# A two-layer sparse-attention step on one core: other places for the threshold rounds, and the softmax reciprocals spread by PE instead of multiplied in by a diagonal

## The chip, the core and the metric

The kernel runs on one core of a Trainium2 chip. Its engines are PE (matrix products; PEld is its weight load), DVE (the vector engine), ACT (the scalar engine, with its function tables), POOL (the general engine) and SP (which issues transfers). Each works through its own list of instructions in order and waits on semaphores that the others raise. The metric is the device time of one execution in microseconds, the median of several.

## The reference

The reference is one step of a two-layer model for a prompt of 528 tokens (16 of them meta tokens) and 8 decoding sequences of 4 tokens with 2048 cached tokens each. The first layer is the one that matters here:

```
s     = einsum(qi, kidx);  score = einsum(relu(s), wi);  score = -inf beyond qpos
idx   = top_k(score, topk)                 # 132 keys of a prompt row, 256 of a decoding row
p     = softmax(q . k[idx] * 64**-0.5);  o = p @ v[idx]      # 8 heads of 64, 2 key heads
y     = concat(o, pooled) @ w_out          # pooled: moving averages over 2, 4, 8, 16 rows
```

A gated feed-forward follows, then a second layer with gated linear attention and another feed-forward. Outputs are the activations, new keys and values, and states.

## The kernel before

All matrix products run in float32 accuracy: each weight slab (RAW) is split into a high part by ACT (`hi`, WHI) and the rest by POOL (`lo`, WLO), and a product is three passes, `tile_rows` (L1820). A slab gives two tiles of 128 output columns, each of 8 steps over the inner dimension; a step is 6 matmuls.

The change lies in the first layer, from some 115 to 350 us of the span, in four stages.

Top-k and slab stage. DVE finds the prompt's top keys by 17 rounds, each of four `top8` (L1324) and four `take8` (L1330), one pair for each block of 112 rows. The decoding rows go another way: a threshold is searched bit by bit, in 32 rounds. A round is a count on DVE (`seek_count`, L1360, over all scores), a sum of the counts over partitions on PE (`row_total`, L1966, one matmul call, two instructions), and an update of the tried bits on DVE (`seek_update`, L1378 and L1380). Round r's count needs the update that reads total r-1. From the top-k round 10 on, DVE's list holds three such rounds in each top-k round (21 in all, `SEEK_EARLY`). At the same time PE works at slabs 4 to 7 (8 tiles, 64 steps), and its list holds total r behind step 3r+2. Ahead of tiles 0 to 5 stand three transposes (`kv_rows`), ahead of tile 6 four others. POOL's splits of slabs 6 and 7 (L607) fall in this stage.

Key phase. For y = 0 to 15, PE turns two chunks of cached keys (`k_turn`, L2010, 8 transposes), and multiplies the chunk turned before with the decoding queries (`k_logits`, L2026); ACT copies the turned keys (L974). Totals 21 to 32 stand one each in y = 1 to 12. Total 33 serves the choice among equal scores (`sample_mask`), and lies behind the first unit's logits; totals from 33 on use another PSUM bank than the others.

Prompt attention. 20 units n = 0 to 19, by descending row block i (n // 4 counts down from block 4 to block 0) and head pair p. A unit has `logits(n)` on PE (L2068), `row_max(n)` on DVE (L1447, adds the mask and takes the maximum), `exps(n)` on ACT (L992, with row sums), `scale_rows(n)` on DVE (L1462 the reciprocals of the sums, L1466 two diagonal matrices INV from identity and reciprocals), `flip(n)` on PE (L2086: each block of probabilities times INV, which turns and normalizes it at once, two instructions a block), `pt_copy(n)` on ACT (L1004), `values(n)` on PE (L2100), `o_hi(n)` on ACT (L1014) and `o_lo(n)` on DVE (L1475). Logits and probabilities are held twice, so units overlap. What overlaps is set by the order written out for each engine:

```
PE   n:  flip(n)  logits(n+2)  sample_masks  values(n)  pooled
ACT  n:  o_hi(n-1)  pt_copy(n)  exps(n+2)  pooled_hi
DVE  n:  scale_rows(n+1)  o_lo(n-1)  row_max(n+2)  pooled_lo  sample_mask  sample_max
```

`pooled` (L2117) and its two halves (`pooled_hi` L1019, `pooled_lo` L1481) are the moving averages' products; they stand in units 4, 5, 7, 8, 10, 11, 13 and 14. The masks of the decoding rows stand in units 12 to 18. POOL makes the moving averages beside this stage (L726 to L739), and its split of the output slab (`lo_at(out0, 0, 0)`, L613) comes behind the fetch of the fifth cached value block.

Of the kernel before, what the change touches and what calls it, by code (L numbers as in the profile page):

```python
# [32 lines left out]
P = 128  # L33
# [49 lines left out]
SEEK_EARLY, SEEK_FROM = 21, 10  # L83
# [12 lines left out]
CUT_STEPS = 5 + 2 * 31 + 3  # L96
# [76 lines left out]
def trunk(nc, t, o):  # L173
# [4 lines left out]
    with ExitStack() as ctx:  # L178
# [78 lines left out]
        INV, _, inv_end = region("INV", [RB, 2, 2, RB], F32, uo_end)  # L257
# [88 lines left out]
        def halved(ap):  # L346
# [22 lines left out]
        tk, nm_ready, nm_final, tks, nms_ready, newscore = (sem(n) for n in ("tk", "nm_ready", "nm_final", "tks", "nms_ready", "newscore"))  # L369
        part_count, row_count = (sem(n) for n in ("part_count", "row_count"))  # L370
        kvr_tr, kvr_ready, ue_tr, sp_ready, uo_ready = (sem(n) for n in ("kvr_tr", "kvr_ready", "ue_tr", "sp_ready", "uo_ready"))
        u_zero, pool_step, pd_ready, y_done, yhi, ylo = (sem(n) for n in ("u_zero", "pool_step", "pd_ready", "y_done", "yhi", "ylo"))
        lg_ready, mx_ready, exp_done, tail_done, p_ready, pt_tr, pt_evac, pv_done, ohi, olo = (
            sem(n) for n in ("lg_ready", "mx_ready", "exp_done", "tail_done", "p_ready", "pt_tr", "pt_evac", "pv_done", "ohi", "olo"))
# [222 lines left out]
        def _(pool):  # L597
# [95 lines left out]
            pool.memset(UE[:, :, 0:PB], 0.0).then_inc(u_zero, 1)  # L693
# [107 lines left out]
        def _(act):  # L801
# [141 lines left out]
            for s in range(6, 8):  # L943
                hi(s + 1)
                for j in range(2):
# [7 lines left out]
                    if g == 0:  # L953
                        act.wait_ge(u_zero, 1)
# [13 lines left out]

            for y in range(16):
# [254 lines left out]
        def _(dve):  # L1224
# [121 lines left out]
            def seek_count(r):  # L1346

                x, junk = SS[:, :], MET[:, :]
                if r == 0:
# [3 lines left out]
                    dve.tensor_tensor(new, new, VNF[3 * NS:P, 0:NS], ALU.mult).then_inc(newscore, 1)  # L1353
                    dve.wait_ge(newscore, 1)
                    dve.tensor_tensor(new, new, VNF[3 * NS:P, NS:2 * NS], ALU.add).then_inc(newscore, 1)
                    dve.wait_ge(newscore, 2)
# [5 lines left out]
            def total(r):  # L1362

                return PS[:, 7 if r < 33 else 1, 0:1]
# [46 lines left out]

            for r in range(1, ROUNDS_P):
# [14 lines left out]
            assert 3 * (ROUNDS_P - SEEK_FROM) == SEEK_EARLY  # L1427
# [29 lines left out]
            def scale_rows(n):  # L1457
# [4 lines left out]
                dve.reciprocal(ST[0:m, 1, 2 * n:2 * n + 2], ST[0:m, 2, 2 * n:2 * n + 2]).then_inc(p_ready, 1)  # L1462
                dve.wait_ge(p_ready, 2 * n + 1)
                if n >= 2:
                    dve.wait_ge(pt_tr, n - 1)
                dve.tensor_tensor(INV[0:m, n % 2, :, 0:m], IDN[0:m, 0:m].unsqueeze(1).to_broadcast([m, 2, m]),  # L1466
                                  ST[0:m, 1, 2 * n:2 * n + 2].unsqueeze(2).to_broadcast([m, 2, m]), ALU.mult).then_inc(p_ready, 1)
# [341 lines left out]
        def _(pe):  # L1809
# [153 lines left out]
            def row_total(r):  # L1963

                pe.wait_ge(part_count, r + 1)
                pe.matmul(PS[:, 7 if r < 33 else 1, 0:1], (PRIOR if r == 33 else SAME)[:, :, :].rearrange("p q n -> p (q n)"), SEEK[:, 2:3], start=True, stop=True).then_inc(row_count, 1)  # L1966
# [526 lines left out]
```

## Time and profile before

| | us |
|---|---|
| median of 3 executions | 1711.35 |
| lowest and highest | 1710.86, 1729.72 |
| the profiled execution's own time | 1712.0 |
| its span, first to last instruction | 1710.2 |
| PE busy in the span | 1589.6 (93%) |
| DVE, ACT, POOL busy | 544.1, 554.1, 549.9 (32% each) |

Shares are of the whole span, over stages with different limits. A row of the timeline gives start, duration, engine, line, operation, and in brackets the idle time ahead of it with what ended it. PEclk is the granted clock of TensorE as a share of 2.4 GHz; 0.50 is its lower level, 1.2 GHz.

### The profile page before, as it was taken

Reading aid. Unit: us, or ns where it says so; the run is one execution under the profiler, and the core shown is the slowest. Engines: PE = TensorE matmul, PEld = TensorE weight load, DVE = VectorE, ACT = ScalarE, POOL = GpSimd, SP = SyncE. Lnnn points to the kernel's source line nnn. Section 1 sums busy time; section 2 is a strip of 40 time slices with the busy share of each in tenths; the row PEclk is TensorE's granted clock in tenths of the full one; section 3 lists DMA queues with packets and bytes.
Section 4 is the critical chain, followed back from the end, with each engine's and each line's share of the span. In section 5 each row is a group of like instructions: output and inputs, shape, how many; then the busy total and the mean of one; then the engine's idle time right before and its main releaser. Section 6 shows DMA issues by size and latency. Waiting matters only on the chain.

```text
span 1710.2 us, 28405 instructions
## 1 busy us (share of the span) xinstructions
PE 1589.6 (93%) x11984; PEld 1484.9 (87%) x11984; DVE 544.1 (32%) x1089; ACT 554.1 (32%) x745; POOL 549.9 (32%) x206
## 2 busy tenths in 40 slices
PE   6896998898999999999889889999989999999996
PEld 6864866578999999999888887789989999999996
DVE  5269855632210101012316772233430111001113
ACT  4243245542432322223344332102333432222231
POOL 5410212513433343333354431002334333434240
PEclk9858998889999999999889987658989999999998
DMA  5322231132222223212221200034212222232221
GB/s 151 130 90 83 71 126 51 48 127 74 72 76 92 74 80 99 94 60 77 82 75 58 67 26 1 1 124 159 75 50 87 85 67 91 87 99 74 71 77 53
DMA packets 116840, 136.04 MB, mean 80 GB/s; under 512 B 5848, under 2 KB 111594, under 8 KB 114705
## 3 DMA queue, kind: packets, MB, share of 16 engines
q1 hardware_dynamic: 112949, 113.91, 21.2%
q0 software_dynamic: 3456, 20.97, 3.5%
q8 instruction: 58, 0.95, 0.2%
q14 instruction: 21, 0.17, 0.0%
q10 hardware_dynamic: 356, 0.03, 0.0%
HBM read 127.14 MB, written 7.94 MB: 79 GB/s over the span
## 4 chain that ended last, share of the span: by engine, by line
PE 84%; DVE 8%; ACT 4%; issue 2%; POOL 0%; ACTq 0%; DMA 0%; DVEq 0%; POOLq 0%
PE PS L1820 66%; PE PS L1917 2%; PE PS L2338 2%; PE PS L2375 2%; PE PS L2336 2%; DVE SC L1330 1%; DVE M L1324 1%; PE PS L2086 1%; PE PS L2370 1%; PE PS L2354 1%; PE PS L2304 1%; PE PS L1848 1%; PE PS L2010 1%; PE PS L2317 1%; DVE BC L1629 1%
## 5 line engine op out<-in xcount | busy, mean ns | idle before, releaser
L1820 PE MATMUL PS<-HHI,WHI 128*128 128x280 f32 x2304 | 647.8, 298 | 19.0 <-DVE HLO L1252 10.8
L1820 PE MATMUL PS<-HLO,WHI 128*128 128x280 f32 x2304 | 641.9, 295 | 0.0
L613 POOL TENSOR_TENSOR WLO<-RAW,WHI 128x2048 fp32r<-128x2048 f32 (+2 forms) x89 | 365.5, 4107 | 780.2 <-ACT WHI L825 590.4
L1820 PE MATMUL PS<-HHI,WLO 128*128 128x280 f32 x2304 | 489.9, 295 | 0.0
L1820 PEld LDWEIGHTS PS<-HHI,WHI 128*128 128x128 f32 x2304 | 444.2, 193 | 24.7 <-issue 14.8
L1820 PEld LDWEIGHTS PS<-HLO,WHI 128*128 128x128 f32 x2304 | 443.6, 193 | 0.0
L1820 PEld LDWEIGHTS PS<-HHI,WLO 128*128 128x128 f32 x2304 | 373.3, 192 | 0.0
L825 ACT ACTIVATE WHI<-RAW 128x2048 fp32r<-128x2048 f32 x87 | 166.1, 1909 | 149.0 <-PE PS L1820 146.0
L1820 PE MATMUL PS<-ALO,WHI 128*128 128x280 f32 x704 | 192.8, 291 | 0.0
L1820 PE MATMUL PS<-AHI,WHI 128*128 128x280 f32 x704 | 192.8, 291 | 0.0
L1595 DVE TENSOR_TENSOR AT<-PS,SG 128x560 f32<-128x560 f32 x44 | 32.6, 742 | 473.7 <-PE PS L1820 473.7
L1820 PE MATMUL PS<-AHI,WLO 128*128 128x280 f32 x704 | 147.5, 291 | 0.0
L1820 PEld LDWEIGHTS PS<-AHI,WHI 128*128 128x128 f32 x704 | 132.5, 188 | 0.0
L1820 PEld LDWEIGHTS PS<-ALO,WHI 128*128 128x128 f32 x704 | 132.3, 188 | 0.0
L1568 DVE TENSOR_TENSOR XT<-PS,XT 128x560 f32 x48 | 35.6, 742 | 298.0 <-PE PS L1820 298.0
L1820 PEld LDWEIGHTS PS<-AHI,WLO 128*128 128x128 f32 x704 | 111.7, 188 | 0.0
L607 POOL TENSOR_TENSOR WLO<-RAW,WHI 128x2048 fp32r<-128x2048 f32 x16 | 75.9, 4747 | 94.2 <-ACT WHI L818 87.8
L1107 ACT ACTIVATE AHI<-AT 128x560 f32 x44 | 29.6, 673 | 224.5 <-DVE AT L1595 224.5
L1102 ACT ACTIVATE SG<-PS 128x560 f32<-128x560 f32 x44 | 28.1, 639 | 147.8 <-PE PS L1820 147.4
L850 ACT ACTIVATE NRM<-XT 128x560 f32 (+1 forms) x32 | 21.5, 672 | 126.4 <-DVE XT L1568 126.2
L818 ACT ACTIVATE WHI<-RAW 128x2048 fp32r<-128x2048 f32 x18 | 34.4, 1911 | 26.2 <-PE PS L1820 24.5
L1917 PE MATMUL PS<-KID,QIT 64*112 64x112 f32 (+3 forms) x128 | 34.7, 554 | 5.8 <-ACT RL L898 5.1
(327 smaller groups left out, 1674.1 us busy)
## 6 DMA issues: line engine op xcount, KB each, us to landing
RAW<-in_ffn_w_gate SPq DMA_DIRECT2D x22, 1024.0 KB, 5.2
RAW<-in_ffn_w_up SPq DMA_DIRECT2D x22, 1024.0 KB, 5.3
RAW<-in_ffn_w_down SPq DMA_DIRECT2D x16, 768.0 KB, 4.7
RAW<-in_w_in_odd SPq DMA_DIRECT2D x12, 1024.0 KB, 5.3
RAW<-in_ffn_w_down SPq DMA_DIRECT2D x16, 640.0 KB, 4.2
RAW<-in_w_in_even SPq DMA_DIRECT2D x7, 1024.0 KB, 5.3
RAW<-in_w_out_even SPq DMA_DIRECT2D x4, 1024.0 KB, 5.2
SIN<-in_state_gla SPq DMA_DIRECT2D x8, 512.0 KB, 3.9
```

The costliest lines, as they stand in the source:

```text
L607: pool.tensor_tensor(WLO[:, s % 2, 0:kc, :], RAW[:, s % 2, 0:kc, :], WHI[:, s % 2, 0:kc, :].bitcast(F32), ALU.subtract).then_inc(lo_done, 1)
L613: pool.tensor_tensor(WLO[:, par, 0:kc, :], RAW[:, par, 0:kc, :], WHI[:, par, 0:kc, :].bitcast(F32), ALU.subtract).then_inc(lo_done, 1)
L818: act.activation(WHI[:, s % 2, :, :], RAW[:, s % 2, :, :], ACT.Copy).then_inc(hi_done, 1)
L825: act.activation(WHI[:, s % 2, :, :], RAW[:, s % 2, :, :], ACT.Copy).then_inc(hi_done, 1)
L1107: act.activation(AHI[:, ds(2 * i + j, 1), :].rearrange("p a n -> p (a n)"), AT[:, j, :], ACT.Copy).then_inc(ahi_ready, 1)
L1568: dve.tensor_tensor(x, halves(j), x, ALU.add).then_inc(acc_free[j], 1)
L1595: dve.tensor_tensor(halved(AT[:, j, :]), halves(j), halved(SG[:, j, :]), ALU.mult).then_inc(acc_free[j], 1)
L1820: ins = pe.matmul(acc[a][:, half, 0:HALF], w[:, slot, k, c0:c0 + P], x[:, k0 + k, HALF * half:HALF * half + HALF], start=first and n == 0 ...
L1917: ins = pe.matmul(PS[0:m, 4 + 2 * (n % 2) + half, 0:nk // 2], QIT[lo:lo + 64, h // 2, RB * i:RB * i + m], KID[lo:lo + 64, half * (nk // 2) ...
L2336: pe.matmul(out, STATE[:, c % 2, h, 128 * e:128 * e + 128], G[:, h, CH * c:CH * c + m], start=True, stop=False)
L2338: ins = pe.matmul(out, VR[rows, c % 2, x:x + 128], ATT[rows, h // 2, CH * c:CH * c + m], start=not inter, stop=True)
L2375: ins = pe.matmul(PS[:, 7, y:y + DT], SIN[:, b % 2, h, 128 * e:128 * e + 128], G[:, h, WP + DT * b:WP + DT * b + DT], start=True, stop=True)
```

## The change

Fourteen threshold rounds stay in the top-k rounds (two in each from round 10 on), and their totals lie further apart in the slab stage; the rest goes to the key phase. The flips become plain transposes, which need the exponentials only. The reciprocals are spread by PE: the column of a head's reciprocals, broadcast to 64 columns, is the weight, the identity streams, and 64 partitions get the reciprocal of each row. DVE copies that to SBUF (`spread`) and multiplies the product of the values with it (`o_norm`), ahead of `o_hi`. Logits of unit n+2 wait until `spread(n)` has read the bank that they share. An Exp on one column is put ahead of the key phase on ACT. POOL's split of the output slab goes behind the last fetch of cached values.

```diff
-SEEK_EARLY, SEEK_FROM = 21, 10
+SEEK_EARLY, SEEK_FROM = 14, 10
+SEEK_STEPS = [7 + 9 * r // 2 for r in range(13)]
+K_TOTALS = [[r for r in range(len(SEEK_STEPS), 33) if (r - len(SEEK_STEPS)) * 4 // 5 == y] for y in range(16)]
@@ gpsimd
-            cached("v", 4)
+            for b in range(4, 8):
+                cached("v", b)
             lo_at(out0, 0, 0)
-            for b in range(5, 8):
-                cached("v", b)
@@ scalar
+            act.activation(STS[:, 0, 0:1], IDN[:, 0:1], ACT.Exp)
             for y in range(16):
...
-                act.wait_ge(pv_done, n + 1)
+                act.wait_ge(o_rows, n + 1)
                 act.activation(HHI[:, p, RB * i:RB * i + m], PS[:, 2, 0:m], ACT.Copy).then_inc(ohi, 1)
@@ vector
                     if r >= SEEK_FROM and i == 3:
-                        seek_round(3 * (r - SEEK_FROM))
+                        seek_round(2 * (r - SEEK_FROM))
                 for i in range(1, NRB):
                     take8(i, 8 * r + i)
-                    if r >= SEEK_FROM and i % 2 == 0:
-                        seek_round(3 * (r - SEEK_FROM) + i // 2)
+                    if r >= SEEK_FROM and i == 3:
+                        seek_round(2 * (r - SEEK_FROM) + 1)
...
+            def row_inverse(n):
+                dve.wait_ge(exp_done, n + 1)
+                dve.reciprocal(ST[0:m, 1, 2 * n:2 * n + 2], ST[0:m, 2, 2 * n:2 * n + 2]).then_inc(rinv, 1)
+            def spread(n):
+                dve.wait_ge(inv_rows, n + 1)
+                if n >= 2:
+                    dve.wait_ge(o_rows, n - 1)
+                dve.tensor_copy(INV[:, n % 2, 0:m], PS[:, 4 + 2 * (n % 2), 0:m]).then_inc(rinv, 1)
+            def o_norm(n):
+                dve.wait_ge(rinv, 2 * n + 2)
+                dve.wait_ge(pv_done, n + 1)
+                dve.tensor_tensor(PS[:, 2, 0:m], PS[:, 2, 0:m], INV[:, n % 2, 0:m], ALU.mult).then_inc(o_rows, 1)
...
-            dve.wait_ge(nm_ready, NRB - 1)
+            sample_left()
+            sample_mask(2)
             row_max(0)
-            sample_left()
             row_max(1)
-            scale_rows(0)
+            row_inverse(0)
             for n in range(len(UNITS)):
-                if n + 1 < len(UNITS):
-                    scale_rows(n + 1)
+                spread(n)
                 if n:
                     o_lo(n - 1)
                 if n + 2 < len(UNITS):
                     row_max(n + 2)
                 if n in POOLED_AT:
                     pooled_lo(*POOLED_AT[n])
-                if n < 4:
-                    sample_mask(2 + n)
+                if n < 3:
+                    sample_mask(3 + n)
                 for k in MASKS_AT.get(n, ()):
                     sample_max(k)
+                if n + 1 < len(UNITS):
+                    row_inverse(n + 1)
+                o_norm(n)
@@ tensor
                         step = KC * tile + k
-                        if step % 3 == 2 and step // 3 < SEEK_EARLY:
-                            row_total(step // 3)
+                        if step in SEEK_STEPS:
+                            row_total(SEEK_STEPS.index(step))
...
-                if 1 <= y <= 32 - SEEK_EARLY + 1:
-                    row_total(SEEK_EARLY + y - 1)
+                for r in K_TOTALS[y]:
+                    row_total(r)
...
                 k_logits(y)
+            pe.wait_ge(tks, CUT_STEPS)
+            row_total(33)
...
-                pe.wait_ge(p_ready, 2 * n + 2)
+                pe.wait_ge(exp_done, n + 1)
...
-                        ins = pe.matmul(PS[0:kb, j // per, c:c + m], PR[0:m, n % 2, x, RB * j:RB * j + kb], INV[0:m, n % 2, x, 0:m], start=True, stop=True)
+                        ins = pe.transpose(PS[0:kb, j // per, c:c + m], PR[0:m, n % 2, x, RB * j:RB * j + kb], ident(m))
+            def inverse_rows(n):
+                pe.wait_ge(rinv, 2 * n + 1)
+                for x in range(2):
+                    ins = pe.matmul(PS[64 * x:64 * x + 64, 4 + 2 * (n % 2), 0:m], ST[0:m, 1, 2 * n + x:2 * n + x + 1].to_broadcast([m, HD]), ident(m), start=True, stop=True)
+                ins.then_inc(inv_rows, 1)
...
             logits(0)
-            row_total(33)
-            pe.wait_ge(tks, CUT_STEPS)
+            pe.wait_ge(tks, LEFT_STEPS)
             logits(1)
-            pe.wait_ge(tks, LEFT_STEPS)
             for n in range(len(UNITS)):
+                inverse_rows(n)
                 flip(n)
                 if n + 2 < len(UNITS):
+                    pe.wait_ge(rinv, 2 * n + 2)
                     logits(n + 2)
```

By these lists `K_TOTALS` puts totals 13 to 32 into y = 0 to 15, two of them in y = 0, 4, 8 and 12 and one in each other y. The rest of the diff renames semaphores and drops one bank choice.

## Rows read from the trace of the kernel before

**Rows 1.** Windows: busy of PE, PEld, DVE, ACT, POOL, then PEclk, DMA share, GB/s.
```profile
225.50:261.50 36.00, 34.87 (x240) 20.17 (x240) 14.44 (x49) 22.65 (x46) 7.78 (x12) 1.00 0.45 154
...
269.50:351.30 81.80, 74.29 (x587) 51.55 (x587) 47.92 (x176) 44.16 (x139) 28.19 (x23) 0.85 0.12 39
```

**Rows 2.** Timeline of PE, slab stage: six of the 21 totals.
```profile
160.07 0.59 PE L1966 MATMUL PS<-SEEK,SAME 128*128 128x1 f32 x2 [5.49 <-DVE MET L1358]
...
170.34 0.28 PE L1966 MATMUL PS<-SEEK,SAME 128*128 128x1 f32 x2
...
172.90 0.28 PE L1966 MATMUL PS<-SEEK,SAME 128*128 128x1 f32 x2
...
176.07 0.28 PE L1966 MATMUL PS<-SEEK,SAME 128*128 128x1 f32 x2
...
182.05 0.59 PE L1966 MATMUL PS<-SEEK,SAME 128*128 128x1 f32 x2 [3.28 <-DVE MET L1360]
...
223.56 0.28 PE L1966 MATMUL PS<-SEEK,SAME 128*128 128x1 f32 x2
```

**Rows 3.** Timeline of DVE and POOL, top-k and slab stage.
```profile
121.44 1.94 DVE L1324 MAX8 M<-SC 112x8 f32<-112x228 f32 x4
...
125.42 1.95 DVE L1324 MAX8 M<-SC 112x8 f32<-112x228 f32 x4
...
176.64 4.53 DVE L1380 SCALAR_TENSOR_TENSOR BITS<-BITS 128x1 int32<-128x1 int32 x1
...
176.62 4.54 POOL L607 TENSOR_TENSOR WLO<-RAW,WHI 128x2048 fp32r<-128x2048 f32 x1 [28.06 <-ACT WHI L818]
```

**Rows 4.** Timeline of PE, DVE and ACT, key phase.
```profile
230.00 0.28 PE L1966 MATMUL PS<-SEEK,SAME 128*128 128x1 f32 x2
...
230.32 0.22 DVE L1378 TENSOR_SCALAR BITS<-PS,SEEK 128x1 int32<-128x1 f32 x1 [5.21 <-PE PS L1966]
...
231.48 0.08 DVE L1360 DVE_READ_ACCUMULATOR MET<-SS,BITS 128x1 f32 x1
...
226.37 1.09 ACT L974 ACTIVATE KTC<-PS 128x512 f32<-128x512 f32 x2 [0.76 <-PE PS L2010]
```

**Rows 5.** Chain that ended last, key phase: start, us, what.
```profile
250.30 0.12 PE PS L1966 x2
...
251.40 1.02 PE PS L2010 x8
```

**Rows 6.** Timeline of ACT, PE and POOL between key phase and unit 0.
```profile
264.69 1.28 ACT L992 ACT_TABLE_LOAD   x1 [3.10 <-DVE ST L1455]
...
269.47 3.78 PE L2086 MATMUL PS<-INV,PR 80*112 80x80 f32 x20 [3.58 <-DVE INV L1466]
...
261.23 1.36 POOL L726 TENSOR_TENSOR PA<-UE 128x694 f32<-128x694 f32 x1
```

**Rows 7.** One line's instructions: the scans of layer two; ns min/median/max.
```profile
L1629 DVE TENSOR_TENSOR_SCAN BC<-CG,BC x4: 1393/3567/5724, 905.4 to 918.1; 128x608 f32<-128x608 f32 x4
```

**Rows 8.** Chain that ended last, units 3 to 7.
```profile
287.24 0.96 PE PS L2068 x4
...
289.44 1.41 ACT PR L992 x4
...
293.67 1.57 PE PS L2086 x16
...
298.86 0.39 ACT HHI L1019
```

**Rows 9.** Timeline of PE and DVE, attention units.
```profile
289.12 1.82 PE L2086 MATMUL PS<-INV,PR 112*112 112x112 f32 x16
...
336.78 1.70 PE L2086 MATMUL PS<-INV,PR 112*112 112x112 f32 x8
...
294.97 0.51 DVE L1481 SCALAR_TENSOR_TENSOR HLO<-PS,COLS,HHI 128x280 fp32r<-128x280 f32 x1 [1.86 <-ACT HHI L1019]
...
325.08 4.00 DVE L1466 TENSOR_TENSOR INV<-CA,ST 112x224 f32<-112x224 f32 x1
```

More of the change, by code:

```diff
@@ L95 @@
 SCOLS = 4 * QCOLS
-CUT_STEPS = 5 + 2 * 31 + 3
+SEEK_STEPS = [7 + 9 * r // 2 for r in range(13)]
+K_TOTALS = [[r for r in range(len(SEEK_STEPS), 33) if (r - len(SEEK_STEPS)) * 4 // 5 == y] for y in range(16)]
+assert sum(K_TOTALS, []) == list(range(len(SEEK_STEPS), 33))
+CUT_STEPS = 7 + 2 * 31 + 3
 LEFT_STEPS = CUT_STEPS + 1
@@ L368, in trunk @@
             sem(n) for n in ("kit_tr", "kit_ready", "ss_done", "sr_done", "comb_done", "comb_evac"))
-        tk, nm_ready, nm_final, tks, nms_ready, newscore = (sem(n) for n in ("tk", "nm_ready", "nm_final", "tks", "nms_ready", "newscore"))
+        tk, nm_ready, nm_final, tks, nms_ready = (sem(n) for n in ("tk", "nm_ready", "nm_final", "tks", "nms_ready"))
         part_count, row_count = (sem(n) for n in ("part_count", "row_count"))
         kvr_tr, kvr_ready, ue_tr, sp_ready, uo_ready = (sem(n) for n in ("kvr_tr", "kvr_ready", "ue_tr", "sp_ready", "uo_ready"))
-        u_zero, pool_step, pd_ready, y_done, yhi, ylo = (sem(n) for n in ("u_zero", "pool_step", "pd_ready", "y_done", "yhi", "ylo"))
-        lg_ready, mx_ready, exp_done, tail_done, p_ready, pt_tr, pt_evac, pv_done, ohi, olo = (
-            sem(n) for n in ("lg_ready", "mx_ready", "exp_done", "tail_done", "p_ready", "pt_tr", "pt_evac", "pv_done", "ohi", "olo"))
+        inv_rows, pool_step, pd_ready, y_done, yhi, ylo = (sem(n) for n in ("inv_rows", "pool_step", "pd_ready", "y_done", "yhi", "ylo"))
+        lg_ready, mx_ready, exp_done, tail_done, rinv, o_rows, pt_tr, pt_evac, pv_done, ohi, olo = (
+            sem(n) for n in ("lg_ready", "mx_ready", "exp_done", "tail_done", "rinv", "o_rows", "pt_tr", "pt_evac", "pv_done", "ohi", "olo"))
         kv_in = [sem(f"kv_in{i}") for i in range(6)]
@@ L953, in _ @@
                     if g == 0:
-                        act.wait_ge(u_zero, 1)
+                        act.wait_ge(pads_set, 4)
                     evac(s, j, UE[:, g, PB:PB + HALF], acc[j][:, 0, 0:HALF], False)
@@ L1352, in seek_count @@
                     dve.wait_ge(casts, 13)
[L1353 to L1356, printed above, removed]
+                    seeking(dve.tensor_tensor(new, new, VNF[3 * NS:P, 0:NS], ALU.mult))
+                    seeking(dve.tensor_tensor(new, new, VNF[3 * NS:P, NS:2 * NS], ALU.add))
                     dve.wait_ge(pads_set, 3)
@@ L1362, in total @@
             def total(r):
-                return PS[:, 7 if r < 33 else 1, 0:1]
+                return PS[:, 7, 0:1]
             def seek_update(r):
@@ L1410, in seek_round @@
                 seek_count(r)
+            assert 2 * (ROUNDS_P - SEEK_FROM) == SEEK_EARLY
             for r in range(1, ROUNDS_P):
@@ L1461, in scale_rows @@
                 dve.wait_ge(exp_done, n + 1)
-                dve.reciprocal(ST[0:m, 1, 2 * n:2 * n + 2], ST[0:m, 2, 2 * n:2 * n + 2]).then_inc(p_ready, 1)
-                dve.wait_ge(p_ready, 2 * n + 1)
-                if n >= 2:
-                    dve.wait_ge(pt_tr, n - 1)
-                dve.tensor_tensor(INV[0:m, n % 2, :, 0:m], IDN[0:m, 0:m].unsqueeze(1).to_broadcast([m, 2, m]),
-                                  ST[0:m, 1, 2 * n:2 * n + 2].unsqueeze(2).to_broadcast([m, 2, m]), ALU.mult).then_inc(p_ready, 1)
+                dve.reciprocal(ST[0:m, 1, 2 * n:2 * n + 2], ST[0:m, 2, 2 * n:2 * n + 2]).then_inc(rinv, 1)
+            def spread(n):
+                i, p = UNITS[n]
+                m, nk = blk(i)
+                dve.wait_ge(inv_rows, n + 1)
+                if n >= 2:
+                    dve.wait_ge(o_rows, n - 1)
+                dve.tensor_copy(INV[:, n % 2, 0:m], PS[:, 4 + 2 * (n % 2), 0:m]).then_inc(rinv, 1)
+            def o_norm(n):
+                i, p = UNITS[n]
+                m, nk = blk(i)
+                dve.wait_ge(rinv, 2 * n + 2)
+                dve.wait_ge(pv_done, n + 1)
+                dve.tensor_tensor(PS[:, 2, 0:m], PS[:, 2, 0:m], INV[:, n % 2, 0:m], ALU.mult).then_inc(o_rows, 1)
             def o_lo(n):
@@ L1965, in row_total @@
                 pe.wait_ge(part_count, r + 1)
-                pe.matmul(PS[:, 7 if r < 33 else 1, 0:1], (PRIOR if r == 33 else SAME)[:, :, :].rearrange("p q n -> p (q n)"), SEEK[:, 2:3], start=True, stop=True).then_inc(row_count, 1)
+                pe.matmul(PS[:, 7, 0:1], (PRIOR if r == 33 else SAME)[:, :, :].rearrange("p q n -> p (q n)"), SEEK[:, 2:3], start=True, stop=True).then_inc(row_count, 1)
             def kv_rows(i):
```

8 lines of the change are left out of this document (4 added, 4 removed).

## The prediction

> **What bounds the kernel now.** I read the page first, then the windows, the chain that ended last, and the engines' timelines of 115 to 351 us; outside that stretch the instructions stay as they are, so whatever the change does there it passes on in full. The stages have different limits. In the slab stage PE is the engine that should be full, yet it waits for the count of DVE: 5.49 us ahead of total 0 and 3.28 us ahead of another [rows 2]. In the key phase PE is busy 34.87 of 36.00 us at a granted clock of 1.00 [rows 1], so every instruction added to PE there is paid. The attention units are a ring over three engines: logits, row maximum, exponentials, and then the next flip [rows 8]; PE is busy in most of it, at a mean clock of 0.85 [rows 1].
>
> **Slab stage: less.** Totals 0 to 20 lie between 160.07 and 223.56 [rows 2], 63.5 us for 20 intervals. A plain interval is 2.56 us (170.34 to 172.90), one with a tile's transposes 3.17 (172.90 to 176.07). Fourteen plain ones, five with transposes and one of some 3.0 (the four turns ahead of tile 6, an estimate) are 54.7. The other 8.8 us are waits and the slow stretches behind them. A total costs 0.12 [rows 5], so a step is (2.56 - 0.12) / 3 = 0.81.
> Now the DVE side of the new order. Two rounds fall into one top-k round of 125.42 - 121.44 = 3.98 us [rows 3], and a round's own work is 1.24 us (230.32 to 231.56) [rows 4]: 3.2 us a round. PE has 4.5 steps and a total, 3.8 us, plus transposes. PE sets the pace, with about half a microsecond to spare in each round.
> Terms: the first total stands behind step 7 and not 2, so five steps, 4.05 us, move into the wait of 5.49, which shrinks to 1.4. Eight totals leave: 1.0. The 8.8 us of waits go, except where POOL's split of a slab holds DVE: the update took 4.53 us beside a split of 4.54 [rows 3], where its work is some 0.2. There are still two splits. Each finds DVE some 1 to 1.5 us ahead, so I keep 0.9. Sum: -13. Bounds: -14 if the slack covers both; -8 if one split holds DVE in full and PE slows behind it, as it did at 182.05 (0.59 for a total that takes 0.28 otherwise).
>
> **Key phase: more.** Twelve totals become twenty: 8 x 0.12 = 1.0 [rows 5]. Four of the y hold two totals back to back, and the second needs the first one's update and count. From a total's start to the end of the count it feeds is 231.56 - 230.00 = 1.56 us [rows 4], with the hand-off 1.6, in which PE, in order, does nothing but 0.12 us of work: 4 x 1.5 = 6.0. No other wait hides it, as PE has hardly any here. The Exp ahead of the phase loads a table, 1.28 us [rows 6], and runs some 0.2; ACT had 0.76 us idle at that place [rows 4], so the first turned keys come 0.7 later, and PE needs them. Sum: +7.7 (between +6 and +9). Total 33 waits for DVE behind the last logits, but ACT's last copies are as late, so I cost it at nothing (up to 0.5 without that cover).
> The Trainium skill (ScalarE: Activation LUTs, What ACT_TABLE_LOAD costs) puts a drain of about 1.38 us on top of each table load. By that the phase would start another 1.4 us later; the row of the load here, with the exponential behind it, shows no such drain.
>
> **Up to unit 0: a little less.** The load of 1.28 us lay beside the second row maximum on DVE, so its place there gains nothing. The diagonal of unit 0, which ended PE's wait of 3.58 us [rows 6], goes; I take 1.5 for it, an estimate, as it lay beside POOL's adds of 1.36 [rows 6], and another took 4.00 beside a longer POOL instruction [rows 9]. Against that a scan now stands ahead of the first row maximum. A scan takes 1.39 us alone and up to 5.72 beside POOL [rows 7], and POOL's first add starts just there: row maximum 0 begins 0.9 us later. Sum: -0.6 (between -2 and +2).
>
> **Attention units: more, against what the flips promise.** A flip of 8 blocks takes 1.57 us as 16 instructions [rows 8]; 8 transposes take 1.02 in the key phase [rows 5], and I take 0.9 for the smaller tiles. Over all units that takes some 12 us of work off PE, to which the spreading products add 20 x 0.25 (an estimate, between 0.2 and 0.5: four instructions at the flip's 0.1 each, or two side by side). What decides is DVE's order. The reciprocals of n+1 now stand behind the pooled half of n. That half needs ACT's, which was the wait of 1.86 us [rows 9]; ACT's stands behind the exponentials of n+2 and needs the product that PE makes last in unit n. And PE has the spreading product of n+1, which waits for the reciprocals, ahead of flip n+1. Before, the reciprocals behind that half were those of n+2, one unit later. So in the eight pooled units nothing of two units overlaps any more. Unit 4, from flip to flip: spreading 0.25, transposes 0.9, logits 0.96, row maximum with hand-offs 1.24 (288.20 to 289.44), exponentials 1.41, pooled halves 0.39 on ACT [rows 8] and some 0.45 of 0.51 on DVE [rows 9], reciprocals and hand-offs 0.35: 5.9 us.
> The eight: 2 x 5.9 with 448 keys; 2 x 5.2 at 336 and 2 x 4.5 at 224 (estimates, by the parts that grow with the keys); 2 x 5.3 for units 13 and 14, which have a mask product too. Sum 41.8; with 3.2 each for units 6, 9 and 12, 51.4, against 336.78 - 289.12 = 47.7 now [rows 9], in which POOL's hold of the diagonal, 4.00 [rows 9], is already gone: +3.7. Units 0 to 3, with the mask steps of DVE ahead of the reciprocals, come to 20.2 against 289.12 - 269.47 = 19.6 [rows 6, 9]: +0.6. The last five gain and lose alike. Sum: +4.3 at the full clock.
> The clock: 0.85 is the mean of the units now [rows 1], and 20 instructions of unit 0 took 3.78 us [rows 6], 0.19 each, behind an idle of 3.58 us, where 16 took 1.57 later on [rows 8]. The new waits, about 2 us a pooled unit, make the same share of lower clock likely. Some 45 us of the chain are PE's; 45 x (1 / 0.85 - 1) = 8. I take 5, as part of today's loss is at the first flips and behind POOL's hold (bounds 0 and 12).
> POOL's split of the output slab moves behind the last product of values. Its 4.5 us (those of the split in [rows 3]) lie beside the decoding rows' flips and value products, which PE does before it reads that slab, so I cost that at nothing; if it were late, up to 4.5 would show.
>
> **The sum.** -13 + 7.7 - 0.6 + 4.3 + 5 = +3.4 on the profiled execution's own 1712.0 (span 1710.2): 1715. That execution lies 0.65 above the median, so the two are the same for this. Two per cent, 34 us, is about what a measurement of this kernel can tell from no change; all terms together stay inside it.
>
> **Rivals.**
> *The units are bound by PE's work, not by DVE's order.* Then the flips' 12 us come off and the holds of the diagonals with them, less 5 for the spreading: some -13 in place of +9.3. For it: PE is busy 74.29 of 81.80 us [rows 1]. Against it: the order as written. Time: 1712 - 13 + 7.7 - 0.6 - 13 = 1693.
> *The clock stays at its lower level through the units*, and the kernel is slower than before. PE's work there is 74.29 x 0.85 = 63 us at the full clock, less 12, plus 5: 56; at 1.2 GHz 112, plus some 1.2 us of hand-offs in each pooled unit: 121 against 81.8, +39. Time: 1712 - 13 + 7.7 - 0.6 + 39 = 1745. It decides where the waits of 2 us, which come back in each unit, keep the clock down; a share of a third already brings +13. For it: 3.78 us for the first flips [rows 6]. Against it: 1.00 in the key phase [rows 1], where 1.02 of each 2.1 us are transposes [rows 5]. The Trainium skill (TensorE: Matmul & The Clock Gate, Part 4: PE-mode transpose) says that transposes don't count as PE being busy; by that rule the new flips speak for this rival, and the key phase, half transposes at full clock, shows that it doesn't hold for such a mix.
> *DVE still paces the slab stage*, because both splits hold it in full: -13 becomes about -4, 1724.
> *The change doesn't do what it says* in one place: rounds leave the top-k, but if PE has no wait there to give back, the stage gains only 5 us: 1723. The row of 5.49 speaks against that.
>
> **How the numbers follow.** Forecast, within 1704 to 1726: 0.70. PE-bound units, 1693: 0.12. Lower clock, 1726 to 1750: 0.11. The two slab cases, 1723 and 1724, where they come with a slower clock and so pass 1726: 0.07. Eight in ten lie between 1699 and 1729. Below 1677 needs the first rival and a key phase without its waits: 0.01. Above 1746 needs the lower clock and a lost slab stage: 0.03.
>
> **What would show it.** Right: the slab stage's totals about 3.8 us apart with no wait over 2 us but the first, slab products ending near 211; PE idle for 1.4 us ahead of the second total of y = 0, 4, 8, 12, and a key phase of 42 to 44 us; in units 4, 5, 7, 8, 10, 11 the flip ended by the reciprocal, and that by the pooled half, 4.5 to 6 us apart. Wrong: units under 4 us with pooled products in them, or PEclk at 0.5 through the units, or waits for DVE in the middle of the slabs.

## The result, and the profile after

The changed kernel took 1735.26 us (median of four, 1732.55 to 1740.85), the kernel before 1712.0 in the same comparison. The ratio is 1.0111, 95% interval 1.0062 to 1.016: slower by about 1%, inside two per cent, 20 us above the forecast of 1715 and 6 us above its range of 1699 to 1729. The profiled execution is the longest of the four, 1740.85 with a span of 1739.0; its stages against those of before:

| stretch | before | after | difference | forecast |
|---|---|---|---|---|
| first total to last slab product | 64.6 | 51.2 | -13.4 | -13 |
| key phase, to its last logits | 36.1 | 45.3 | +9.2 | +7.7 |
| from there to flip 0 | 8.65 | 9.67 | +1.0 | -0.6 |
| attention units, flip 0 to the last product of values | 81.8 | 105.7 | +23.8 | +4.3 +5 |
| everything behind | 1358.9 | 1367.0 | +8.1 | 0 |

The windows of the changed kernel (busy us of each engine with its instructions, then the granted clock), beside [rows 1]:

```profile
160.00:211.34 51.34, 51.20 (x381) 49.63 (x381) 46.21 (x138) 13.99 (x33) 10.16 (x3) 0.97 0.19 60
...
211.30:256.65 45.35, 37.07 (x257) 22.42 (x257) 25.30 (x86) 24.26 (x48) 7.50 (x11) 1.00 0.38 130
266.32:290.00 23.68, 18.66 (x160) 12.55 (x159) 11.29 (x46) 9.91 (x32) 1.61 (x2) 0.64 0.01 1
290.00:310.00 20.00, 16.14 (x124) 9.91 (x123) 7.82 (x32) 10.77 (x30) 7.66 (x7) 0.82 0.01 1
310.00:330.00 20.00, 15.64 (x110) 9.60 (x106) 7.58 (x33) 9.27 (x29) 9.28 (x8) 0.74 0.00 1
330.00:350.00 20.00, 16.68 (x80) 8.00 (x77) 7.17 (x35) 7.72 (x25) 2.36 (x3) 0.53 0.15 53
350.00:371.99 21.99, 18.54 (x87) 8.18 (x87) 10.57 (x51) 8.96 (x30) 1.88 (x2) 0.50 0.28 96
266.32:371.99 105.67, 85.66 (x545) 48.24 (x544) 44.43 (x195) 46.64 (x143) 22.79 (x22) 0.65 0.09 31
```

In the slabs PE is now busy 51.20 of 51.34 us. In the units the mean clock is 0.65 where it was 0.85, and from 330 us on PE works at its lower level, 1.2 GHz, nearly throughout. It has fewer instructions than before (545 for 587 in the whole stage), yet is busy 85.66 us where it was 74.3.

One pooled unit of the changed kernel in the timeline (start, duration, engine, line, in brackets the idle time and what ended it), in place of [rows 8]:

```profile
290.46 0.98 PE L2103 MATMUL PS<-CA,PR 112*112 112x112 f32 x8
...
293.64 0.67 ACT L995 ACTIVATE PR<-PR,ST 112x448 f32<-112x448 f32 x1 [1.19 <-DVE ST L1448]
...
294.95 0.47 ACT L1022 ACTIVATE HHI<-PS,COLS 128x280 fp32r<-128x280 f32 x1
295.46 0.51 DVE L1494 SCALAR_TENSOR_TENSOR HLO<-PS,COLS,HHI 128x280 fp32r<-128x280 f32 x1 [1.86 <-ACT HHI L1022]
295.88 0.15 DVE L1463 RECIPROCAL ST<-ST 112x2 f32<-112x2 f32 x1
...
296.09 0.41 PE L2112 MATMUL PS<-CA,ST 112*64 112x112 f32 x4 [1.93 <-DVE ST L1463]
296.44 0.79 PE L2103 MATMUL PS<-CA,PR 112*112 112x112 f32 x6
```

This is the chain that the prediction wrote down: exponentials, pooled half on ACT, pooled half on DVE, reciprocals, spreading product, flips, 5.98 us from flip to flip where 5.9 was forecast. PE stands idle for 1.93 us in it. Over the stage its waits, by what ended them, are:

```profile
PE PS L2112 <- DVE ST L1463: 18.3, 14, 1.9
PE PS L2126 <- ACT PT L1007: 1.5, 4, 0.4
```

That is 18.3 us in 14 waits for the reciprocals, none longer than 1.9. These are the waits foreseen. What was priced too low is what they do to the clock.

The key phase and the way to flip 0, in the timelines of PE, ACT and DVE of the changed kernel:

```profile
214.24 0.66 PE L2025 MATMUL PS<-CA,KNN 128*128 128x128 f32 x4 [0.89 <-ACT KTC L977]
...
226.38 0.28 PE L1981 MATMUL PS<-SEEK,SAME 128*128 128x1 f32 x2
227.99 0.38 PE L1981 MATMUL PS<-SEEK,SAME 128*128 128x1 f32 x2 [1.33 <-DVE MET L1361]
228.31 1.05 PE L2041 MATMUL PS<-KTC,QBD 128*32 128x512 f32 x4
...
230.22 0.28 PE L1981 MATMUL PS<-SEEK,SAME 128*128 128x1 f32 x2
230.43 1.05 PE L2041 MATMUL PS<-KTC,QBD 128*32 128x512 f32 x4
...
255.23 0.38 PE L1981 MATMUL PS<-SEEK,SAME 128*128 128x1 f32 x2 [1.09 <-DVE MET L1389]
...
261.31 0.39 PE L2082 MATMUL PS<-KT,QT 64*80 64x80 f32 x1 [2.72 <-DVE ST L1456]
...
212.21 1.28 ACT L971 ACT_TABLE_LOAD   x1
213.50 0.20 ACT L971 ACTIVATE STS<-CA 128x1 f32<-128x1 f32 x1
...
257.23 2.22 DVE L1396 TENSOR_TENSOR_SCAN NTH<-MET 128x544 f32<-128x544 bf16 x1
259.48 0.62 DVE L1448 CUSTOM_DVE_ANT_0 PR<-PS,NM 80x448 f32<-80x448 f32 x1
...
263.41 0.62 DVE L1448 CUSTOM_DVE_ANT_0 PR<-PS,NM 80x448 f32<-80x448 f32 x1 [2.24 <-PE PS L2088]
...
264.94 0.79 DVE L1456 TENSOR_TENSOR ST<-ST 80x2 f32<-80x2 f32 x1
```

In four pairs the second total waits 1.33 us, the turned keys come 0.89 late behind the table load, and total 32 waits 1.09 for a count that starts with the change of sign of the scores. A single total holds the logits behind it until 0.21 us after its own start (230.22 to 230.43), a pair until 1.93 after the start of the first (226.38 to 228.31), so a second total costs 1.72 in all.

The row maxima of units 0 and 1 and the second logits in the kernel before, for the way to flip 0:

```profile
262.93 0.62 DVE L1447 CUSTOM_DVE_ANT_0 PR<-PS,NM 80x448 f32<-80x448 f32 x1 [7.13 <-issue]
...
266.03 0.62 DVE L1447 CUSTOM_DVE_ANT_0 PR<-PS,NM 80x448 f32<-80x448 f32 x1 [1.36 <-PE PS L2071]
...
264.76 0.26 PE L2065 MATMUL PS<-KT,QT 64*80 64x80 f32 x1 [1.68 <-DVE SEEK L1432]
```

The last row of the table is a stage that the change doesn't touch. Nearly all of it lies in one stretch, first in the kernel before, then in the changed one:

```profile
1011.67:1124.72 113.05, 108.23 (x586) 87.62 (x585) 32.11 (x72) 28.12 (x48) 4.51 (x1) 0.75 0.03 10
```

```profile
1032.04:1152.79 120.75, 115.94 (x586) 93.54 (x585) 32.09 (x72) 28.09 (x48) 4.51 (x1) 0.69 0.03 9
```

These are the same 586 products at a clock of 0.69 for 0.75. In the profiled runs below the part behind the units takes between 1355.0 and 1367.0 us, and no edit touches it; 5.6 us of the 8.1 are the distance of this execution from its median. So stages are compared below, and totals beside them. Without that row the terms sum to +20.6, and 1712.0 + 20.6 is 1732.6, as long as the fastest of the four executions took.

### The profile page after: what moved, and what is told of

Its sections match the earlier page's. It is cut to its first block, busy times and chain, and to the rows that moved or that the text cites. A ratio compares the mean times of both kernels' runs of the same rounds, so it can differ in the third digit from the quotient of the medians.

```text
span 1739.0 us, 28383 instructions
## 1 busy us (share of the span) xinstructions
PE 1605.4 (92%) x11944; PEld 1484.3 (85%) x11944; DVE 541.9 (31%) x1109; ACT 555.6 (32%) x746; POOL 550.2 (32%) x206
## 4 chain that ended last, share of the span: by engine, by line
PE 85%; DVE 8%; ACT 3%; issue 2%; DMA 1%; POOL 0%; SPq 0%; DVEq 0%; ACTq 0%; POOLq 0%
PE PS L1835 65%; PE PS L2364 2%; PE PS L1932 2%; PE PS L2362 2%; PE PS L2401 2%; PE PS L2085 1%; DVE SC L1333 1%; DVE M L1327 1%; PE PS L2103 1%; PE PS L2380 1%; PE PS L2396 1%; PE PS L2330 1%; PE PS L2025 1%; PE PS L2343 1%; PE PS L1863 1%
## 5 line engine op out<-in xcount | busy, mean ns | idle before, releaser
L2364 PE MATMUL PS<-ATT,VR 64*128 64x64 f32 (+1 forms) x160 | 39.8, 371 | 0.9 <-DVE G L1744 0.9
```

The costliest lines, as they stand in the source:

```text
L2364: ins = pe.matmul(out, VR[rows, c % 2, x:x + 128], ATT[rows, h // 2, CH * c:CH * c + m], start=not inter, stop=True)
```

## The experiments

There are three theories for the 23.8 us of the units. One: DVE's order, reciprocals of n+1 behind the pooled half of n, makes PE wait, and the waits bring the lower clock. Two: the transposes keep the clock down whatever the waits. Three: the ring through PE, DVE and PE is longer, at any clock. All profiled stages together (times in us, the units with the mean clock in them; ratio against the kernel before with its 95% interval):

| run | key phase | to flip 0 | units (clock) | behind | median | ratio |
|---|---|---|---|---|---|---|
| before | 36.1 | 8.65 | 81.8 (0.85) | 1358.9 | 1712.0 | |
| after | 45.3 | 9.67 | 105.7 (0.65) | 1367.0 | 1735.3 | 1.0111 [1.0062, 1.016] |
| e1 order | 45.4 | 8.25 | 82.0 (0.83) | 1360.4 | 1714.3 | 1.000 [0.9974, 1.0026] |
| e2 products | 45.4 | 9.67 | 120.8 (0.70) | 1365.5 | 1755.7 | 1.0234 [1.0197, 1.027] |
| e3 both | 45.4 | 9.67 | 93.2 (0.79) | 1366.0 | 1726.3 | 1.0058 [1.0035, 1.0081] |
| e4 filler | 45.4 | 8.27 | 92.6 (0.99) | 1356.7 | 1721.4 | 1.0058 [1.0035, 1.008] |
| e12 order, filler | 48.3 | 9.49 | 88.5 (0.96) | 1359.7 | 1714.5 | 1.0016 [1.0001, 1.003] |
| e5 even, units of before | 41.1 | 10.12 | 86.9 (0.77) | 1361.1 | 1703.3 | 0.9943 [0.9907, 0.9978] |
| e6 the same, filler | 41.1 | 10.12 | 81.1 (0.95) | 1355.0 | 1703.9 | 0.9937 [0.9907, 0.9967] |
| e7 even, order, filler | 41.8 | 8.38 | 87.2 (0.87) | 1363.8 | 1710.5 | 0.9945 [0.9905, 0.9986] |
| e8 even, later half, filler | 41.1 | 9.66 | 80.1 (0.96) | 1361.2 | 1702.5 | 0.9925 [0.9893, 0.9956] |
| e9 sixteen rounds | 39.9 | 8.64 | 81.0 (0.96) | 1362.0 | 1706.3 | 0.9944 [0.9914, 0.9975] |
| e10 flips first | 39.9 | 6.97 | 86.1 (0.92) | 1361.9 | 1709.4 | 0.9943 [0.991, 0.9976] |
| e11 sixteen, units of before | 39.9 | 9.27 | 83.9 (0.92) | 1357.8 | 1703.7 | 0.9889 [0.9825, 0.9954] |

The stages come from one execution of each kernel, the median and the ratio from all of them. Those executions of e1 and e4 lie 5 and 6 us below their medians, that of e5 lies 10 above.

**e1, DVE's order alone.**

```diff
                 if n + 2 < len(UNITS):
                     row_max(n + 2)
+                if n + 1 < len(UNITS):
+                    row_inverse(n + 1)
                 if n in POOLED_AT:
                     pooled_lo(*POOLED_AT[n])
...
-                if n + 1 < len(UNITS):
-                    row_inverse(n + 1)
                 o_norm(n)
```

> The changed kernel, with one thing moved: on DVE the reciprocals of n+1 stand ahead of the pooled half, the mask steps and the decoding maxima of n, directly behind row maximum n+2. The stage from the first flip to the last product of values took 81.8 us before and 105.6 us after the change. Theory 1 (DVE's order makes PE wait, and the waits bring the lower clock): the waits of PE for the reciprocals, 18 us in the stage, fall under 6, the granted clock of 330 to 372 us rises from 0.5 to over 0.8, and the stage takes 78 to 88 us. Theory 2 (the plain transposes keep the clock down, whatever the waits): the waits go, but the clock stays at its lower level in the second half: 90 to 98 us. Theory 3 (the longer ring through PE, DVE and PE again is what costs): 98 to 106 us, with the waits of PE now for the copied spread.

The stage takes 82.0 us: 23.7 of the 23.8 are gone, and the medians of the two kernels lie 21.0 apart. The stage in the windows of this run, and PE's waits in it:

```profile
330.00:350.00 20.00, 17.90 (x92) 9.02 (x91) 11.78 (x53) 9.15 (x29) 4.48 (x4) 0.62 0.36 114
265.09:347.09 82.00, 69.69 (x545) 39.88 (x544) 44.28 (x195) 45.19 (x143) 24.13 (x23) 0.83 0.12 39
```

```profile
PE PS L2085 <- DVE INV L1472: 8.6, 9, 1.2
PE PS L2112 <- DVE ST L1463: 1.6, 3, 0.8
```

The same 545 products take PE 69.69 us busy and not 85.66. The waits for the reciprocals fall from 18.3 to 1.6, but a new one stands behind them: 8.6 us in which logits wait for the copied spread, as DVE does that behind the pooled half. The clock of the last units was expected above 0.8 and is lower (0.62 in 330 to 350): the length of the stage is the one that theory one gave, and that part of its expectation missed.

**e2 and e3, products with the identity in place of transposes.**

```diff
-                        ins = pe.transpose(PS[0:kb, j // per, c:c + m], PR[...], ident(m))
+                        ins = pe.matmul(PS[0:kb, j // per, c:c + m], PR[...], ident(m), start=True, stop=True)
```

> The changed kernel, with the flips as products with the identity (two instructions a block) in place of transposes; the order on every engine is that of the change. Theory 1 (order and waits): the waits stay, so does the lower clock, and PE has some 12 us more to do at full clock: the stage takes 108 to 125 us. Theory 2 (transposes keep the clock down): the granted clock of 330 to 372 us rises to over 0.8, and the stage takes 88 to 96 us, shorter than 105.6 although PE has more to do. Theory 3 (longer ring): 106 to 112 us, at whatever clock.

> Both edits together: the reciprocals earlier on DVE, and the flips as products with the identity. Theory 1: the waits are gone, the clock is at 0.85 or more, and the stage takes 82 to 90 us, somewhat more than with the order alone, as the products cost PE more than the transposes. Theory 2: 80 to 88 us at a high clock, and clearly less than with the order alone. Theory 3: 95 us or more.

First e2, then e3, in their windows:

```profile
350.00:387.22 37.22, 31.95 (x144) 17.30 (x143) 14.36 (x70) 12.57 (x41) 1.89 (x2) 0.50 0.17 59
266.44:387.22 120.78, 100.10 (x665) 66.34 (x664) 44.42 (x195) 46.65 (x143) 22.83 (x22) 0.70 0.08 27
```

```profile
267.13:360.30 93.17, 87.58 (x665) 58.49 (x664) 44.45 (x195) 46.05 (x143) 22.80 (x22) 0.79 0.10 35
```

Without a single transpose in the units the clock is again at 0.50 from 350 us on, its mean is 0.70 for 0.65, and the stage is 15.1 us longer, where theory two wanted it 10 to 18 shorter at over 0.8. Theory two falls. By the rule of the Trainium skill (TensorE: Matmul & The Clock Gate, Part 4: PE-mode transpose), that transposes don't count as PE being busy in the same way, the clock should have risen well above that here; this kernel doesn't bear it out. e3 against e1 gives the price of products instead of transposes with the order mended: 93.2 - 82.0 = 11.2 us (12.0 between the medians), which the forecast had as 12. And e3 against before, both with products for flips and early reciprocals, puts the hop by PE and a copy at 93.2 - 81.8 = 11.4. Both differences hold some of the clock too, as the three stages ran at 0.79, 0.83 and 0.85. No theory had e3 right: theory one wanted 82 to 90 us at 0.85 or more, theory three 95 or more. Theory three, which also wanted 98 or more in e1, does not hold for the 23.8, but its hop isn't free: in these runs it takes about what the transposes save.

**e4 and e12, filler for the clock.**

```diff
             for n in range(len(UNITS)):
+                if n:
+                    pe.wait_ge(pt_evac, n)
+                for _ in range(10):
+                    pe.matmul(PS[:, 0, 0:256], IDB[:, :], EXB[:, :, :].rearrange("p g n -> p (g n)"), start=True, stop=True)
                 inverse_rows(n)
```

> The changed kernel, with ten bf16 products of 256 columns ahead of each unit's spreading product on PE, into the bank that the flip is about to write. They do nothing for the result and add some 1.1 us of work at full clock to each unit, most of it in the time in which PE waits for the reciprocals. If the lower clock is what costs (theory 1 in its second half, and theory 2): the granted clock of 330 to 372 us rises to over 0.8 and the stage gets shorter than 105.6 in spite of 22 us more work: 86 to 96 us. If the ring itself costs (theory 3), or if the clock does not answer to PE's work: 106 to 125 us.

> The changed kernel with the reciprocals earlier on DVE and the same ten idle products a unit as the run that had filler alone (92.6 us at 0.99). The two differ in DVE's order only and should both hold the full clock, so the difference is what the order costs in the ring itself, with no help of the clock: by the forecast's unit periods, 5 to 9 us, so 84 to 88 us here. If the order costs by the clock alone, 91 to 93; if it costs by the ring alone, some 70 (the 23.7 us of the first experiment).

e12 is e4 with the edit of e1. The whole stage of e4 and its stretch from flip 0 to flip 17 (18 units), then that stretch in e12:

```profile
264.18:356.82 92.64, 83.35 (x735) 52.01 (x734) 43.69 (x195) 46.59 (x143) 24.10 (x23) 0.99 0.10 35
...
264.18:348.20 84.02, 75.65 (x682) 48.17 (x680) 39.58 (x174) 44.05 (x134) 23.17 (x22) 0.99 0.08 26
```

```profile
270.85:348.00 77.15, 74.64 (x682) 47.77 (x681) 39.65 (x174) 43.69 (x134) 22.04 (x21) 1.00 0.08 29
```

With some 25 us of idle work added (1.27 us for ten of the products, 20 units) the units of the change get 13 us shorter, 105.7 to 92.6, at a clock of 0.99, inside the 86 to 96 expected; the medians lie 13.8 apart. The clock is thus a cause, and its price at least 13 us. In the controlled pair, 682 products each and a full clock in both, the order alone costs 84.02 - 77.15 = 6.9 us; the medians of e4 and e12 are 7.0 apart. That is also a lower bound, as PE is busy 74.64 of 77.15 us in e12, so that there the filler lies on its path. So at least 7 of the 23.8 us are ring and at least 13 are clock; the 4 that are left these runs don't divide. In e12 the clock fell in the last two units, so its whole stage of 88.5, just above the 84 to 88 expected, is no clean figure; its key phase ran at 0.93 and took 48.3, the one run in which that phase was not at full clock.

**e5 to e8, even totals, and who is late next.**

```diff
-K_TOTALS = [[r for r in range(len(SEEK_STEPS), 33) if (r - len(SEEK_STEPS)) * 4 // 5 == y] for y in range(16)]
+K_TOTALS = {}
+for r in range(len(SEEK_STEPS), 33):
+    at = round(3.1 * (r - len(SEEK_STEPS)))
+    at += at % 4 == 3
+    K_TOTALS.setdefault(divmod(at, 4), []).append(r)
...
-            act.activation(STS[:, 0, 0:1], IDN[:, 0:1], ACT.Exp)
...
+                for r in K_TOTALS.get((y, 0), ()):
+                    row_total(r)
                 if y + 1 < 16:
                     k_turn(2 * y + 2)
+                for r in K_TOTALS.get((y, 1), ()):
+                    row_total(r)
+                if y + 1 < 16:
                     k_turn(2 * y + 3)
-                for r in K_TOTALS[y]:
+                for r in K_TOTALS.get((y, 2), ()):
                     row_total(r)
```

> The rounds of the change with the attention units of the kernel before (flips as products with the scaled diagonal, reciprocals and diagonal as they stood), and two edits to the key phase: the twenty totals stand evenly between its turns and logits, three or four pieces of PE's work apart, in place of two in a row in four of the passes; and the exponential ahead of the phase is left out, so that the table is loaded at the first exponential of unit 0 again. If the second total of a pair waits for its own round (my forecast's +6), the phase takes 37 to 39 us instead of 45.4, and it starts 0.7 earlier; if the rounds of DVE are what the phase lacks time for, wherever the totals stand, it stays over 43. The units take 81.8 us again, give or take 3 for the clock, as they don't depend on the rounds. In all about -13.4 + 1.8 + 0 on before: 1700 (1696 to 1706); 1707 or more if the even totals bring nothing.

> The kernel of the run before this one, with four idle bf16 products of 256 columns ahead of each unit's flips on PE. It tells what the units of the kernel before take at the full clock. If the lower clock costs them what their mean of 0.85 suggests (some 8 to 11 us of PE's 74), the stage takes 72 to 78 us at a clock of 0.97 or more, though PE has 9 us more to do; if PE's work or DVE's diagonals bound it anyway, 80 to 88.

> The changed kernel with the reciprocals earlier on DVE (as in the first experiment), the even totals, and six idle bf16 products ahead of each unit; the exponential ahead of the key phase stays. At the full clock the ring of the reordered units should take 72 to 78 us (its PE work of 70 us was done at a mean clock of 0.83, and 12 us were waits); if the copied spread behind the pooled half is what remains, 78 to 84. Against the changed kernel with filler alone (92.6 us at 0.99) the difference is what DVE's order costs without any help of the clock. The key phase starts 0.7 to 1.5 us later than in the runs without that exponential.

> As the run before this one, with the pooled half of n on DVE behind the spread of n+1 (one unit later) and without the exponential ahead of the key phase. If the logits of a pooled unit wait for the copied spread because that stands behind the pooled half (1.1 to 1.4 us in each of eight units in the first experiment), the stage is 5 to 9 us shorter than in the run before: 66 to 73 us. If another engine is late next, the two are within 2 us. In all, with -13.4 in the slabs and +2 in the key phase: 1688 to 1696, faster than both kernels.

e8 moves the pooled half on DVE behind the next spread:

```diff
                 if n:
                     o_lo(n - 1)
+                if n - 1 in POOLED_AT:
+                    pooled_lo(*POOLED_AT[n - 1])
                 if n + 2 < len(UNITS):
                     row_max(n + 2)
...
-                if n in POOLED_AT:
-                    pooled_lo(*POOLED_AT[n])
```

The key phase of e5 in PE's timeline and windows:

```profile
216.93 0.38 PE L1969 MATMUL PS<-SEEK,SAME 128*128 128x1 f32 x2
217.17 0.64 PE L2013 MATMUL PS<-CA,KNN 128*128 128x128 f32 x4
...
218.64 0.38 PE L1969 MATMUL PS<-SEEK,SAME 128*128 128x1 f32 x2 [0.40 <-DVE MET L1363]
```

```profile
212.57:253.68 41.11, 38.33 (x257) 21.84 (x257) 25.12 (x86) 23.14 (x46) 7.50 (x11) 1.00 0.40 134
```

4.3 us come back, less than the 6.4 to 8.4 expected. The pairs' waits of 1.33 are now 0.40 in four places, and a total costs 0.24 (216.93 to 217.17) where the forecast had 0.12: with logits on one side and a turn on the other, more than between two turns' products (0.17). The median of 1703.3 is in the range expected. The units are not: 86.9 us at 0.77 for 81.8 give or take 3, as the first four ran at the lower clock, in an execution 10 us above the median. Leaving out the early exponential is no gain: the phase is 41.1 long for 41.8 with it (e7), and flip 0 comes 9.66 to 10.12 us later for 8.38.

In the units e6, with the old flips and filler, takes 81.1 at 0.95, and e8, with the new ones, 80.1 at 0.96. From flip 1 on both are at the full clock and take nearly the same, first e6, then e8:

```profile
271.00:344.34 73.34, 68.83 (x613) 47.38 (x612) 41.74 (x164) 42.96 (x136) 21.73 (x20) 1.00 0.13 44
```

```profile
269.75:343.51 73.76, 70.03 (x611) 41.29 (x610) 41.21 (x182) 42.42 (x134) 21.20 (x20) 1.00 0.13 44
```

So with clock and order mended the spreading by PE shows no gain. But e8 has six idle products a unit and e6 four, which is some 5 us more in 19 units at 1.27 for ten; what the two would take with the same filler is not shown. The expectations for e6, e7 and e8 were lower (72 to 78, 72 to 84, 66 to 73, and 1688 to 1696 for e8's total): filler was thought to lie in waits alone, and part of it is on PE's path, so that e6 at 0.95 gains nothing on before's 81.8 at 0.85. In e7 the clock fell again, and its stage took 87.2; its windows, and then the whole stage of e8:

```profile
310.00:330.00 20.00, 18.53 (x137) 9.81 (x133) 10.65 (x52) 10.10 (x34) 3.46 (x5) 0.97 0.31 104
330.00:350.00 20.00, 19.13 (x84) 9.14 (x83) 7.91 (x36) 6.97 (x21) 3.09 (x3) 0.50 0.19 60
```

```profile
263.37:343.51 80.14, 76.41 (x659) 45.91 (x658) 44.11 (x195) 45.38 (x143) 22.81 (x22) 0.96 0.12 41
```

With the same filler e7 lost the clock near 329 us, and then PE was busy 19.13 of 20.00 us and did not get it back. e8 kept it. From flip 0 to flip 14, at nearly the same clock (0.97 and 0.95), the two take 60.7 and 60.5 us, so the pooled half's later place is worth little or nothing by itself; behind flip 14 e7 takes 6.8 us longer, at 0.65 where e8 is at 1.00.

**e9 to e11, sixteen rounds in the top-k.**

```diff
-SEEK_EARLY, SEEK_FROM = 14, 10
+SEEK_EARLY, SEEK_FROM = 16, 9
...
-SEEK_STEPS = [7 + 9 * r // 2 for r in range(13)]
+SEEK_STEPS = [6 + 4 * r for r in range(15)]
```

> The units of the run with the pooled half one unit later and filler, the scan back behind the first mask steps of unit 0, and sixteen rounds in the top-k from round 9 on (totals at step 6 and every fourth step of the slabs), so that eighteen totals are left for the key phase, spread evenly. If a total in the key phase costs PE what the last run shows between two kinds of work (some 0.25 us) plus 0.4 of wait wherever two stand under 1.8 us apart, three fewer give 38.5 to 40 us in place of 41.1, and the slabs stay within 1 us of 52. With the scan out of the way, flip 0 starts 7 to 8 us after the last key logits instead of 9.7. In all 1693 to 1699. If DVE can't keep the pace of 3.5 us in the slabs, those grow by 3 to 6 us and nothing is gained.

> As the run before this one, with the flips of a unit ahead of its spreading product on PE. If the spreading product's wait for the reciprocals still holds back the flips, the units get 2 to 6 us shorter (74 to 78 us at the full clock); if the logits behind both are what the next unit needs, they stay within 1.5 us of the run before.

> The sixteen rounds, even totals and scan of the two runs before this one, with the attention units of the kernel before and four idle products a unit, which were 81.1 us at 0.95. It tells whether the spreading by PE is worth anything once order and clock are the same: if the 11 us that the longer ring costs and the 11 us that the transposes save cancel, as the first three experiments say, the units are 79 to 82 us and the total within 3 us of the run with the flips behind the spreading product.

The key phase falls to 39.9 as expected, but the slab products end no earlier for it (212.7 in e9, 212.6 in e8), and the total doesn't fall: e9's 1706.3 is above the 1693 to 1699 expected, and its ratio is no better than e8's. Flip 0 comes 8.64 us behind the key phase, with the scan out of the way, where 7 to 8 was expected. Flips ahead of the spreading product gain nothing: at a clock of 1.00 in both, flip 16 comes 68.9 us behind flip 0 in e10 and 66.5 in e9. e10's stage of 86.1, for the 74 to 78 or at most 1.5 more than e9 expected, lost the clock at the end again. e11, with the units of before, is 83.9 at 0.92 for the 79 to 82 expected, its first two units mostly at the lower level; its total is within 3 us of e9's, as expected.

The best are e8, e5, e6 and e11, at 0.989 to 0.994 of the kernel before (0.994 to 0.995 by the medians): all faster than both kernels, than the one before by under 1.2%, and not told apart by these runs. What they share is fourteen or sixteen rounds in the top-k with even totals; three of them have the old units.

## Why the prediction was wrong, by its own steps

**Slab stage.** Right. -13.4 for -13. The wait for total 0 shrank to 1.85 us (forecast 1.4), and PE is full behind it.

**Key phase.** Right in mechanism and sign, 9.2 for 7.7, just beyond its bound of 9. The second totals cost 4 x 1.72 = 6.9, work and wait together (forecast 6.0 and their share of the 1.0 for eight totals), the table load 0.89 (0.7). Missing was total 32's 1.09, a wait that the forecast looked for only at total 33. No drain of 1.38 us behind the table load shows: the load ends at 213.49 and the exponential starts at 213.50.

**Up to unit 0.** +1.0 for -0.6, inside its bounds. The scan in front took 2.22 us beside POOL's adds and put row maximum 0 0.7 us later behind the key phase (2.8 for 2.1), for 0.9. What the sum lacked is that the second logits ran at the lower clock (2.10 us from their start to row maximum 1, for 1.27), that the last step of that maximum took 0.79 beside a POOL add, for 0.18, and that unit 0 has a spreading product ahead of its flip too (265.86 to 266.32).

**Attention units at the full clock.** Right in mechanism, and near in size where the runs show it. The unit periods of e4 at 0.99 stand beside those of the forecast: the eight pooled ones 6.0, 6.0, 5.4, 5.2, 4.7, 4.7, 5.5 and 5.3, 42.8 for 41.8; units 0 to 3 20.0 for 20.2. Units 6, 9 and 12 take 4.5, 3.9 and 4.2 for 3.2, with 1.27 of filler in front. That filler stands ahead of the other units too: where PE would have waited it costs nothing, elsewhere it is part of the period, so that the closeness is in part luck. The +4.3, the change against the kernel before at the full clock, has no run that shows it cleanly, as the units of before reached the full clock only with filler; the 6.9 is the order's price alone. The hop was probably underpriced: 5 us of products, where e3 shows 11.4 for products, copy and waits together, at a clock of 0.79 against 0.85.

**The clock.** This is the step that failed: the term for it, "I take 5", with bounds 0 and 12. The runs show at least 13. The 5 assumed that new waits bring the *share* of lower clock that the old ones brought, so it was scaled from a mean of 0.85. The runs show two levels between which small things decide: with 18.3 us of waits in pieces under 2 us the stage runs at 0.65, with them gone at 0.83, with them filled at 0.99. And at the lower level PE takes longer (a logits product of 448 columns 0.95 us for 0.54), so the other engines' waits shift too. The mean of one kernel was no price for the next. The total missed by more than this term: slabs, key phase and way to flip 0 were 2.7 us off together, and 8.1 lie in a stage that the change doesn't touch.

**The rivals.** "The clock stays at its lower level" had the mechanism and its place (waits of 2 us, unit after unit). Its size was too high: it gave +39 for the lower level throughout and +13 for a third of that, where the units grew by 23.8 with some seven tenths of the stage at the lower level (a mean of 0.65 between 0.5 and 1). It got 0.11 and should have been level with the forecast, as nothing in the profile of before spoke against it but the key phase, where PE hardly waits. The Trainium skill's page on TensorE (TensorE: Matmul & The Clock Gate, Part 1, the section on a second failure mode) says that short idles between groups of products make the clock swing between its levels; that rule, and not the one on transposes, is what the trace agrees with: 14 waits of up to 1.9 us, 0.65. "PE's work bounds the units" (1693) fell: by e1 and e3 the transposes saved 11.2 us of the stage, but the hop took as much, and PE waited 18.3.

## What to carry to other kernels

When a change adds short waits to PE in a ring that already spends part of its time at the lower clock, price the stage at both levels and give the lower one a real chance; a term scaled from today's mean clock was too small here. An instruction that feeds PE belongs on its engine ahead of any that waits for PE's own later results: here one call moved on DVE was worth 23.7 us of the stage. Spread dependent rounds evenly along PE's other work, since two in a row pay the whole round trip (1.33 us of wait here, 0.40 when spread).

## What was not expected of the hardware

Idle products can pay: some 25 us of them made a stage 13 us shorter, with the granted clock at 0.99 for 0.65.

The lower level holds while PE is busy in the records. In the changed kernel it does so without a gap for 8 us, and in e5, in the first four units, for 28.6:

```profile
318.00:326.00 8.00, 8.00 (x48) 5.20 (x50) 2.96 (x14) 3.22 (x10) 7.59 (x6) 0.50 0.01 2
```

```profile
263.80:292.40 28.60, 28.60 (x184) 22.95 (x185) 11.10 (x43) 9.40 (x30) 1.15 (x2) 0.50 0.00 1
```

What brings it back in one stretch and not in another is open; the busy times here are modelled and may hide gaps.

A one-column product with fp32 weights of 128 by 128 costs 0.24 us between logits and a turn in e5, twice the 0.12 of the chain in [rows 5].
